# The DeltaNet groups of a decoder trunk: from TensorE transposes to a DMA exchange with VectorE block transposes

## The reference, cut to what matters

```python
h = rms_norm(x, norm1_g[l]);  proj = h @ w_in[l]
qkv_g, z, b_logit, a_logit, q_s, k_s, v_s, gate_logits = jnp.split(proj, split_points, axis=-1)
# gdn_branch: conv over time (4 taps per channel), silu, l2 norm, chunked delta rule, norm, gate
qkv_c = jax.nn.silu(causal_depthwise_conv(qkv, conv_w));  q, k, v = jnp.split(qkv_c, 3, axis=-1)
sol = lax.linalg.triangular_solve(a_low + jnp.eye(CHUNK), rhs, ...)      # per chunk of 64
def step(state, inp):                                                    # 4 chunks in order
    v_new = u_n - w_n @ state
    o_n = q_n @ state + qk_n @ v_new
    state = state * d_n + k_n.T @ v_new
o = rms_norm(o, norm_g) * jax.nn.silu(z)
x = x + (g_gdn * (o @ w_branch_gdn) + g_swa * (swa(q_s, k_s, v_s) @ w_branch_swa)) @ w_out
x = x + jnp.square(jax.nn.relu(rms_norm(x, norm2_g) @ w_ff_up)) @ w_ff_down
```

## Time and profile before

| | us |
|---|---|
| median of 3 runs | 1778.62 (1778.43 to 1779.21) |
| profiled execution, its own time | 1778.71 |
| its span, first to last instruction | 1776.5 |
| TensorE busy | 1764.1 |
| VectorE busy | 1265.1 |
| ScalarE busy | 854.7 |
| one window (four in the kernel) | 117.47 |

### The profile page before, as it was taken

The page is one execution under the profiler, slowest core; times in us unless marked ns, Lnnn a source line. Parts: engine busy times, 40 slices in busy tenths (PEclk is TensorE's granted clock), DMA queues, the critical chain, the costliest instruction groups (busy, mean ns, idle before and its releaser), DMA issues.

```text
span 1776.5 us, 27178 instructions
## 1 busy us (share of the span) xinstructions
PE 1764.1 (99%) x9994; PEld 1435.2 (81%) x9994; DVE 1265.1 (71%) x1911; ACT 854.7 (48%) x1353; POOL 97.0 (5%) x82
## 2 busy tenths in 40 slices
PE   9999999999999999999999999999999999999998
PEld 8887777777877888888888888888888888888886
DVE  5578687787886677775667787888644468886444
ACT  6454554554635454554444455544433444544443
POOL 0021030130310000000000000000000000000000
PEclk9999999999999999999999999999999999999999
DMA  8543444444435545445666565556665555556554
GB/s 286 170 158 134 148 154 143 144 144 141 153 121 166 184 154 167 154 154 183 207 204 206 196 213 190 191 194 195 201 195 195 191 194 195 190 189 201 189 191 141
DMA packets 89031, 316.50 MB, mean 178 GB/s; under 512 B 9968, under 2 KB 11648, under 8 KB 88800
## 3 DMA queue, kind: packets, MB, share of 16 engines
q1 hardware_dynamic: 87184, 310.94, 53.3%
q0 software_dynamic: 880, 3.24, 0.6%
q10 hardware_dynamic: 864, 0.87, 0.1%
HBM read 312.92 MB, written 2.10 MB: 177 GB/s over the span
## 4 chain that ended last, share of the span: by engine, by line
PE 92%; DVE 6%; issue 1%; ACT 1%; POOL 0%; POOLq 0%; ACTq 0%
PE acc L359 29%; PE acc L360 28%; PE acc L361 28%; DVE cT L1268 2%; DVE w_lo L1237 1%; PE J L573 1%; PE J L625 1%; PE J L458 1%; PE J L451 1%; PE J L482 1%; PE J L587 1%; PE J L502 0%; PE J L597 0%; PE J L644 0%; PE J L492 0%
## 5 line engine op out<-in xcount | busy, mean ns | idle before, releaser
L1237 DVE TENSOR_TENSOR w_lo<-raw,w_hi 128x1024 fp32r<-128x1024 f32 x582 | 709.9, 1226 | 341.6 <-ACT w_hi L823 338.6
L823 ACT ACTIVATE w_hi<-raw 128x1024 fp32r<-128x1024 f32 x582 | 615.0, 1063 | 640.9 <-PE acc L361 638.2
L359 PE MATMUL acc<-w_hi,hT_hi 128*128 128x512 f32 x1432 | 573.0, 400 | 1.5 <-DVE w_lo L1237 1.5
L360 PE MATMUL acc<-w_lo,hT_hi 128*128 128x512 f32 x1432 | 558.7, 390 | 0.0
L361 PE MATMUL acc<-w_hi,hT_lo 128*128 128x512 f32 x1432 | 558.0, 390 | 0.0
L359 PEld LDWEIGHTS acc<-w_hi,hT_hi 128*128 128x128 f32 x1432 | 268.7, 188 | 66.0 <-issue 7.0
L361 PEld LDWEIGHTS acc<-w_hi,hT_lo 128*128 128x128 f32 x1432 | 268.8, 188 | 57.2
L360 PEld LDWEIGHTS acc<-w_lo,hT_hi 128*128 128x128 f32 x1432 | 269.1, 188 | 52.3 <-issue 1.0
L359 PE MATMUL acc<-w_hi,act_hi 128*128 128x512 f32 x512 | 199.2, 389 | 0.0
L360 PE MATMUL acc<-w_lo,act_hi 128*128 128x512 f32 x512 | 199.2, 389 | 0.0
L361 PE MATMUL acc<-w_hi,act_lo 128*128 128x512 f32 x512 | 199.2, 389 | 0.0
(11 more groups left out here) (247 smaller groups left out, 1369.6 us busy)
## 6 DMA issues: line engine op xcount, KB each, us to landing
raw<-weights SPq DMA_DIRECT2D x582, 512.0 KB, 3.4
xres<-x POOLq DMA_DIRECT2D x4, 512.0 KB, 4.8
xres<-x SPq DMA_DIRECT2D x3, 512.0 KB, 8.5
raw<-weights SPq DMA_DIRECT2D x4, 256.0 KB, 5.1
fgain_sb<-fgain SPq DMA_DIRECT2D x1, 1024.0 KB, 5.5
y<-nat SPq DMA_DIRECT2D x6, 128.0 KB, 2.3
masks_sb<-masks POOLq DMA_DIRECT2D x1, 704.0 KB, 5.0
xres<-x SPq DMA_DIRECT2D x2, 256.0 KB, 4.4
```

What stands on the lines that cost most here:

```text
L359: mm(o, aT_hi[:, kt, tok], w_hi[:, c % RING, w], start=first, stop=False)
L360: mm(o, aT_hi[:, kt, tok], w_lo[:, c % RING, w], start=False, stop=False)
L823: A(w_hi[:, slot], raw[:, slot], ACT.Copy).then_inc(hi_ready, 1)
L1237: tt(w_lo[:, slot], raw[:, slot], w_hi[:, slot].bitcast(F32), ALU.subtract).then_inc(lo_ready, 1)
```

## The change

All seven turns of a group leave TensorE. A turn is now made of 32x32 block transposes by VectorE (one instruction of 128x1024) and an exchange of the blocks between partitions by DMA: the data is written to a buffer in DRAM, and read back so that block rows land on other partitions.

- **Front turns (k, q, v).** ScalarE copies both token tiles out of `acc` with the columns in another order (`by_quarter`); SP writes the slot of `rawg` to DRAM (512 KB), reads it back in eight DMAs of 64 KB with pieces of 512 B; VectorE transposes the blocks (`take_front`) into `rawg`. The taps then read SBUF, not PSUM.
- **Back turns (k, q, v)** and the **output's turn**: VectorE transposes the blocks (`back_turn`, `DVE_OT`), SP writes 512 KB and reads it back in four DMAs of 128 KB with pieces of 1 KB (`quarters`). ScalarE takes k, q and v from the buffers; the scaling of v moves from VectorE to ScalarE (`ACT_VB`). The output is taken up a window later (`OG_AT`), by VectorE in eight pieces where there were four.
- **Tables.** All steps move forward. A group's front part runs within its own window now, beside the last steps of the group before. SP's program for the windows is written out step by step (`groups`), with the exchange's DMAs between the weight chunks.

```diff
-PE_FRONT = {ITEM_K: -8, ITEM_Q: 17, ITEM_V: 54}
-PE_BACK = {ITEM_K: 17, ITEM_Q: 49, ITEM_V: 80}
-PE_ROWS, PE_KK, PE_KQ, PE_QT, PE_OT = 11, 29, 46, 82, 124
+PE_ROWS, PE_KK, PE_KQ, PE_QT = -4, 19, 30, 58
...
+DVE_FRONT = {ITEM_K: -37, ITEM_Q: -25, ITEM_V: -9}
+DVE_BACK = {ITEM_K: -16, ITEM_Q: -3, ITEM_V: 8}
+OG_AT = (86, 86, 86, 66)
+SP_OUT, SP_BACK = (16, 23, 31), (18, 26, 33)
+SP_K, SP_Q, SP_V, SP_O, SP_DIST = (0, 3), (5, 7), (14, 16), (36, 38), 4
...
+            def front_write(k):
+                w, n = divmod(k, 3)
+                sp.wait_ge(rawg_done, 4 * w + n + 1)
+                if k > 1:
+                    sp.wait_ge(front_T, k - 1)
+                sp.dma_start(bounce[k % 2], slot(n)).then_inc(front_out, 16)
...
+            def front_read(k):
+                sp.wait_ge(front_out, 16 * (k + 1))
...
+                for p in range(P // Q):
+                    for t in range(NT):
+                        sp.dma_start(fronts[k % 3 % 2][p * Q:(p + 1) * Q].rearrange("j (t q f) -> j t q f", t=NT, q=P // Q)[:, t],
+                                     kept[:, p, t]).then_inc(front_in, 16)
...
+            def quarters(dst, kept, done):
+                for to in range(P // Q):
+                    sp.dma_start(dst[to * Q:(to + 1) * Q].rearrange("i (r f) -> i r f", r=P // Q),
+                                 kept.rearrange("(r i) (p f) -> i p r f", i=Q, p=P // Q)[:, to]).then_inc(done, 16)
...
+            def turn_back(c, g):
...
+                if c == SP_Q[0]:
+                    sp.wait_ge(q_T32, g + 1)
+                    sp.dma_start(q_bounce, slot(ITEM_Q)).then_inc(q_out, 16)
+                if c == SP_Q[1]:
+                    sp.wait_ge(q_out, 16 * (g + 1))
...
+                    quarters(q_rows, q_bounce, q_in)
...
-            def turn_group(src, b0, sem_, dst_cols=None):
-                for m in range(HG):
-                    for t in range(NT):
-                        ins = tr(J[:, b0 + m // 2, (m % 2) * T + t * P:(m % 2) * T + (t + 1) * P],
-                                 src[:, t, m * P:(m + 1) * P], ident)
-                ins.then_inc(sem_, 1)
...
-                    ins = stt(out=dst[:, m, s:T], in0=J[:, b, o:o + T - s], scalar=cwg[:, n, m, 3 - s:4 - s],
+                    ins = stt(out=dst[:, m, s:T], in0=front(n)[:, m, 0:T - s], scalar=cwg[:, n, m, 3 - s:4 - s],
...
+            def take_front(n, g):
+                k = 3 * g + n
+                dve.wait_ge(front_in, 16 * 8 * (k + 1))
+                V.transpose(front(n).rearrange("p m (b j) -> p b m j", j=Q),
+                            fronts[n % 2].rearrange("p (b m i) -> p b m i", m=HG, i=Q)).then_inc(front_T, 1)
+            def back_turn(a, n, done):
+                V.transpose(slot(n).rearrange("p (r u i) -> p r u i", r=P // Q, u=U),
+                            a.rearrange("p (u r j) -> p r u j", r=P // Q, u=U)).then_inc(done, 1)
...
-                            ts(rawg[:, n, 1], acc[:, n % 2, 1], row_scale(0, 1), None, ALU.mult).then_inc(rawg_d, 1)
```

More of the change, by code:

```diff
@@ L224, in hybrid_trunk, with by_quarter, by_head, front @@
         kdup = rawg[:, 0]
+        def by_quarter(a):
+            return a.rearrange("p (q m i) -> p m q i", q=P // Q, m=HG)
+        def by_head(a):
+            return a.rearrange("p (m q i) -> p m q i", q=P // Q, m=HG)
+        def front(n):
+            return rawg[:, n].rearrange("p t n -> p (t n)").rearrange("p (h t) -> p h t", h=HG)
+        def slot(n):
+            return rawg[:, n].rearrange("p t n -> p (t n)")
+        def unit(rows, u):
+            return rows.rearrange("p (q u i) -> p u q i", q=P // Q, u=U)[:, u]
+        def of_unit(a):
+            return a.rearrange("p (q i) -> p q i", q=P // Q)
+        def o_rows(g):
+            return xres[:, 1, U * P:] if g < NG - 1 else rawg[:, ITEM_V].rearrange("p t n -> p (t n)")
         def mat(i):
@@ new lines, in groups @@
+            def groups(a, b):
+                for c in range(a, b):
+                    for g in range(NG):
+                        turn_back(c - 4 * CPO * (g + 1), g)
+                    for n in range(3):
+                        for w in range(NG):
+                            if c == 4 * CPO * w + SP_OUT[n]:
+                                front_write(3 * w + n)
+                            if c == 4 * CPO * w + SP_BACK[n]:
+                                front_read(3 * w + n)
+                    sp.wait_ge(lo_ready, c - RING + 1)
+                    sp.dma_start(raw[:, c % RING], weights[c]).then_inc(raw_in[c % RING], 16)
@@ L713, in window @@
                 for n in range(4):
-                    free = [] if w == 0 and n < 2 else [(rawg_a, 4 * w + (n - 1)), (rawg_d, 4 * w + (n - 1))]
+                    free = [] if w == 0 and n < 2 else [(rawg_done, 4 * w + (n - 1))]
                     start = w == 0 and n == 0
@@ L723, in fine @@
                     gdn_step(s, w - 1)
[L724 removed]
+                    gdn_step(s - HALVES, w)
                 return fine
             opening()
[L728 removed]
+            window(0, decay_step, lambda s: gdn_step(s - HALVES, 0))
             for w in range(1, NG):
@@ L1083, in ops @@
                             act.wait_ge(r_x, 3)
+                        if q0:
+                            act.wait_ge((k_out, q_out, v_out, silu_done)[n], (4 if n == ITEM_Z else 16) * (q0 // CPO))
                         if n == ITEM_Z:
@@ L1350, in gdn_step @@
                     tt(uq, uq, over(eye64, U), ALU.add).then_inc(u0_ready, 1)
-                for s in (1, 2, 3):
-                    if h == DVE_TAPS[ITEM_Q][s - 1]:
-                        tap(ITEM_Q, s, g, qnT)
-                if h == DVE_SILU[ITEM_Q]:
-                    dve.wait_ge(tanh_done, 4 * g + 2)
-                    silu(qU, qnT)
-                for lv in range(LEVELS - 2):
+                for lv in range(LEVELS):
                     if h == DVE_W[lv]:
@@ L1695, in _ @@
                 q = (OUT_SWA + n) * (CPO // RING)
-                output(q, lambda h: gdn_step(h, NG - 1), read(q + CPO // RING, ops), h0=16 * n)
+                output(q, last_step, read(q + CPO // RING, ops), h0=16 * n)
             for j in range(4):
```

325 lines of the change are left out of this document (171 added, 154 removed).

## The result

The changed kernel takes 1767.81 us in the median of 4 runs (1766.88 to 1768.51) against 1778.53 of the kernel before: ratio 0.994, interval 0.9927 to 0.9952. It is 10.7 us faster, where 21.6 were forecast. The time lies at the upper end of the range; the gain is just under half of what was predicted.

What follows compares the result with a forecast made beforehand. TensorE, running nearly without a gap, was taken as the bound: 1778.7 - 24.6 (turns) - 1.7 (silu wait) + 3 (joint stalls) + 2 (stalls elsewhere) = 1757.4, forecast 1757 us; range 1751 to 1768, chance 0.8.

Steps and rivals of the forecast that it cites:

- where VectorE is tight: VectorE feeding TensorE: new stalls of 1 us per joint, 3 in all, and 0.5 per group elsewhere, 2 in all.
- What leaves TensorE: 224 small matmuls, 28 blocks of 0.88 us, all on the path: 24.6 us, plus 1.7 waiting for k's silu.
- The price of a block transpose: On VectorE, a 128x1024 block transpose takes 1.22 us, seven per group 8.5, bounds 7.9 and 12.5.
- The taps: VectorE's taps, reading SBUF instead of PSUM: four take 1.34 us, upper bound 1.56; 0 to 2 us less per group.
- The second rival: VectorE becomes the bound at the joints, with transposes at 1.78 and taps at 1.56: 1769 or 1766 us; chance 0.22.
- The third: The exchange brings v or q late to VectorE; from 6.5 us stall per window no gain, at 9 1787; chance 0.08.
- The write of q at no cost: On SP, q's write waits for VectorE ahead of chunk 5's weights, covered by k's inner products: 0 us.
- a sign against itself: The forecast is wrong if, among other signs, ScalarE waits for weights by several us.
- DMA share 0.7, window 111 to 113, waits of 3 to 8 us: Signs for the forecast: DMA share near 0.7, window of 111 to 113 us, TensorE's `w_lo` waits 3 to 8 in total.

Runs made afterwards that it cites:

- e4: The kernel before the change with each of its 28 turns made twice, the same values written again: 1801.66 us.
- e1: Changed kernel in which GpSimd's eight mask products per group multiply only 4 of 64 columns and set the rest to zero: 1760.65 us.
- e7: Changed kernel with GpSimd multiplying 4 of 64 mask columns and the second taps of q and v doing one head of four: 1761.08 us.
- e8: Changed kernel with GpSimd's products whole and the second taps of q and v doing one head of four: 1768.72 us.
- e2: Changed kernel with VectorE's front transpose of v at step -6 where it stood at -9: 1769.53 us.
- e9: Changed kernel with SP's write and read of q at chunks 8 and 10 (5 and 7 before), ScalarE's squares of q at step 20 (11 before): 1768.11 us.
- e5: Changed kernel with five of GpSimd's mask products per group given to VectorE, all values kept: 1765.58 us.
- e11: Changed kernel with the edits of e5, e9 and e10 together, all values kept: 1763.56 us.
- e15: e11 with ScalarE's tanh of q at step -7 where it stood at -9, all values kept: 1762.22 us.
- e10: Changed kernel with SP's read of k's rows ahead of one more weight load, ScalarE's first tap of v and squares of k one step earlier: 1768.32 us.

## Which step of the prediction failed, and what of it held

The step that failed is the one on where VectorE is tight, the + 3 + 2 of the sum: VectorE's instructions beside GpSimd's products were given the length that they have alone. The rest of the sum held.

- **What leaves TensorE, 24.6 + 1.7 us:** right. No turn is left, e4 prices them at 23.2, and with these terms the sum closes on the profiled run to about 1 us.
- **The price of a block transpose, 1.22:** right. The groups of VectorE's instructions in the changed kernel have

```profile
L1396 DVE STREAM_TRANSPOSE rawg<-kq 128x1024 f32<-128x1024 f32 x8 | 9.9, 1237 | 0.0
L1391 DVE STREAM_TRANSPOSE rawg<-og_hi 128x1024 f32<-128x1024 f32 x8 | 9.9, 1235 | 4.4 <-DMA og_hi<-bounce 4.3
```

- **The taps, 1.34 per four from SBUF:** wrong by a little where they run undisturbed (223.09 - 221.52 = 1.57, the upper bound), by 2.3 us where GpSimd runs beside them.
- **Where VectorE is tight, 3 us at the joints and 2 elsewhere:** this step failed. It counted VectorE's instructions at the length that they have alone, and took GpSimd only as something to wait for. The stalls that the change adds were put at 5 us and are about 13. A joint, put at 1 us, has 2.3 to 2.9 us of waits. Of the 11.0 us of added waits 8.4 go when GpSimd no longer reads beside VectorE (e1). What is left then, 2.6 us of waits in six stalls more than before, some 4.3 with 0.28 each, is about the 5 that were forecast, and e1's profiled execution, 1758.90, stands 1.5 us from the sum's 1757.4 (its median 3.2). It also put the tight stretch at three joints; all four groups have it, the one of window 1 too, with no older group ahead of it.
- **The second rival, VectorE as the bound at 1766:** near the time, for another reason; that the time lies in the stated range is due to the part drawn for this rival, and so is luck. Its two conditions, transposes at 1.78 and every tap at 1.56, gave it volume. The taps came to 1.57 where undisturbed, the transposes to 1.24, and e7 and e8, with 2.4 us less volume per window, gained nothing in the median.
- **The third, the exchange too late:** VectorE does wait for `front_in` (10.7 and 4.3 us), but e2 shows that moving past v's wait costs more than it gives, and TensorE's first wait for `w_lo` comes 11 us or more behind the end of any of these waits. No added stall could be laid to it. (In the prediction 24 us over 3.5 windows are 6.9 us of stall per window, not 6.5.)
- **The write of q at no cost:** not settled. SP waits there up to 7.8 us. ScalarE's waits for weights, which the prediction had named as a sign against itself, are there (20.9 us in 16). e9's waits are 1.4 us lower with the write moved, but its time is not.
- **DMA share 0.7, window 111 to 113, waits of 3 to 8 us:** the first right (0.71), the others 114.5 and 12.5.

## What to carry to other kernels

When an operand moves from PSUM to SBUF, or a table shifts VectorE's work, lay VectorE's two-input instructions and GpSimd's products on one time axis, and look in the trace for instructions longer than others of their shape: busy time that grows without more instructions is the mark. GpSimd's rows of the kernel before (1.84 for 1.30) would have shown it ahead of the change. An operation given from GpSimd to VectorE can pay although VectorE then has more to do (e5 in the median; e11 and e15, with tables changed too, clear of the spread). And a gain on the bounding engine has to be checked against the chain that feeds it, ScalarE's and VectorE's queues together, since work off one alone moved no median here (e7, e9, e10).

## What the runs showed of the hardware

- VectorE and GpSimd exclude each other when both read two tensors from SBUF: four taps of 1.66 us take 3.73 beside products of 1.30, and such a product up to 2.27; in the kernel before a product behind a `w_lo` takes 1.84. Transposes, reads from PSUM and GpSimd's own memset (0.49) were not involved.
- TensorE's granted clock fell to 1.2 GHz for seven products after some stalls (2.71 us in e8, 3.08 in e7, 1.75 in e10) and not after others (1.77 in the changed kernel, 2.27 in e8), at 1.4 us each time. A stall can so cost more than its length, and not every time; what decides it stays open.
- The exchange's transfers land later than the nearest rows of before suggested: 64 KB reads in pieces of 512 B 3.6 to 3.9 us behind their issue in the median, the 512 KB writes of the front 5.0; 2.3 and 3.3 had been taken.
